# Running sums of squares: which of two engines adds them, in a two-layer decoder trunk

## The chip, the core and the metric

The kernel runs on one core of a Trainium2 chip. The metric is the device time of one launch in microseconds (us). A core has five engines with instruction streams of their own: PE (TensorE, the matmuls), DVE (VectorE), ACT (ScalarE), POOL (GpSimd) and SP (SyncE, which here only issues transfers). Each executes its own instructions in order, and they meet only at semaphores: an instruction raises a counter when it ends, and another engine waits until the counter has reached a number.

## The reference, cut to what matters

The input x has 512 tokens of 1024 features, and there is a memory of 256 tokens. Both layers do the following, where every `rms_norm` divides each token by the root of the mean of its 1024 squares (plus 1e-6) and multiplies by a gain:

```python
for l in range(2):
    h = rms_norm(x, norm_mix_pre[l])             # "mix_pre"
    y = concat(mla(h), mlstm(h), dilated_swa(h)) @ w_out[l]
    x = x + rms_norm(y, norm_mix_post[l])        # "mix_post"
    h = rms_norm(x, norm_x_pre[l])               # "x_pre"
    y = memory_cross_attention(h, rms_norm(mem, norm_mem[l]), x_w_q[l], x_w_kv[l], x_w_o[l])
    x = x + rms_norm(y, norm_x_post[l])          # "x_post"
    h = rms_norm(x, norm_ffn_pre[l])             # "ffn_pre"
    y = swiglu(h, w_gate_up[l], w_down[l])
    x = x + rms_norm(y, norm_ffn_post[l])        # "ffn_post"
```

The six norms with a name in the comments are the ones of this case, in two layers: twelve norms of 1024 features.

## The kernel before, in words

**Layout.** Activations are kept feature-major: x is eight tiles (KT = 8) of 128 features (the partitions) by 512 tokens. Every weight matrix comes as units of 128 x 1024 f32 (512 KB), 128 units per layer, through a ring of four buffers (RING = 4). For each unit SP loads `raw`, ACT writes a rounded copy `w_hi` (L872), DVE writes the rest `w_lo` = raw - w_hi (L1207), and PE makes three matmuls per product (hi by hi, hi by lo, lo by hi: L504 to L506). A unit's `w_hi` can be written once PE has used the unit four before it. Activations are split in the same way into `h_hi` (ACT) and `h_lo` (DVE).

**The sum of squares of a norm.** For each of its eight tiles ACT squares the tile into `sq`, which has two buffers (`square`, L886 to L891). Before it writes one, it waits until the square two before has been added (`squares_added`, L890). DVE keeps the running sum `acc` (`add_square`, L1179 to L1189): a copy for the first tile (L1186) and an addition of two 128 x 512 f32 tiles in SBUF for the other seven (L1188). DVE then waits for its own result (`done`). When all eight are in, PE multiplies `acc` by a matrix of ones, which sums over the features (`norm_sum`, L545 to L552), and ACT makes `rstd` of it with a logarithm and an exponential (`make_rstd`, L900 to L909).

**Where the twelve sums stand.** In each layer:

- "mix_post" is summed while PE makes the eight tiles of the output projection ("out"); DVE norms the memory in the same loop (L1559). PE's `norm_sum` stands behind the first tile of the next projection ("xk").
- "x_pre": when rstd of mix_post is there, DVE scales a tile of y (L1267) and adds the tile before to x (L1271), then makes one `w_lo` (L1565), then adds the square of the tile before that (L1567). PE meanwhile makes the xk tiles and the first four units of "xv" with matmuls of 256 columns or with two token blocks; `norm_sum("x_pre")` stands behind the fourth xv unit (L793). ACT, in its own order for tile m (L1120 to L1126): `w_hi` of unit m + 3, `k_x` of tile m, the square of tile m - 3. The `w_hi` of the fourth xv unit comes behind the last square (L1127).
- "x_post" is summed during the eight tiles of "xo", and "ffn_post" during the eight of "down". In both PE's `norm_sum` stands directly behind the last tile (L821, L856), and four matmuls without use follow (`keep_busy`, L563), save at the kernel's end.
- "ffn_pre" (`ffn_input`, L1597) and, for the second layer, "mix_pre" (`next_input`, L1633) follow them: per tile DVE does y (L1267), x (L1271), `h_lo` of the tile before (L1194), the square's addition. PE takes each tile as soon as its `h_lo` is there (`after_norm`, L568): 12 matmuls per tile in front of ffn_pre, 9 in front of mix_pre (L580 to L582).

**The other users.** In the feed-forward part `acc` and `sq` hold other data (L328). POOL does nothing in the kernel but one copy per layer (L495), which it makes when the last numerator of the mLSTM has been computed.

Of the kernel before, what the change touches and what calls it, by code (L numbers as in the profile page):

```python
# [23 lines left out]
DEPTH = 2  # L24
# [232 lines left out]
def build(nc, x_in, mem_in, w_in, g_in, c_in, out):  # L257
    with ExitStack() as ctx:
# [199 lines left out]
        with nc.Block() as block:  # L458
# [31 lines left out]
            @block.gpsimd  # L490
            def _(pool):
                for layer in range(DEPTH):
                    pool.wait_ge(k_pe_ready, count(k_pe_ready, layer, 1))
                    pool.wait_ge(ml_num, count(ml_num, layer, ML_HEADS * TB))
                    pool.tensor_copy(k_mla[K_PE_ROWS[0], 2:MLA_HEADS, :], k_pe[K_PE_ROWS[0], :].unsqueeze(1)  # L495
                                     .broadcast_to([MLA_ROPE, MLA_HEADS - 2, SEQ])).then_inc(k_pe_copied, 1)

            @block.tensor
# [674 lines left out]
            def _(dve):  # L1173
# [5 lines left out]
                def add_square(layer, name, k):  # L1179

                    c = layer * N_SQUARES + squares_before(name) + k
                    dve.wait_ge(squared, c + 1)
                    if k == 0:
                        if layer or NORM_AT[name]:
                            dve.wait_ge(norm_summed, count(norm_summed, layer, NORM_AT[name]))
                        ins = dve.tensor_copy(acc[:, :], sq[:, c % 2, :])  # L1186
                    else:
                        ins = dve.tensor_tensor(acc[:, :], acc[:, :], sq[:, c % 2, :], ALU.add)  # L1188
                    done(ins, squares_added)  # L1189
# [30 lines left out]
                for layer in range(DEPTH):  # L1220
                    def gain(col, rows=slice(0, P)):
                        return gains[rows, layer, col:col + 1]

                    def add_squares(name, n, between=None, beside=lambda k: None):
                        for k in range(n):
                            beside(k)
                            add_square(layer, name, k)
                            if between is not None:
                                between(k)
# [314 lines left out]
                    for s in range(PAIR_STEPS + PAIR_LAG + 2):  # L1544
# [9 lines left out]
                        if t >= 2 and t % TB == 1:  # L1554
# [3 lines left out]
                    mem_norm = (KT, tiles(mem), G_MEM, tiles(m_hi), tiles(m_lo))  # L1558
                    add_squares("mix_post", KT, between=lambda m: norm_step("mem", m, *mem_norm),  # L1559
                                beside=lambda m: lo_until(U_OUT + m + 4))  # L1560
                    norm_step("mem", KT, *mem_norm)
                    
                    def x_square(k):

                        lo_until(U_XK + k + 4)  # L1565
                        if k >= 1:
                            add_square(layer, "x_pre", k - 1)  # L1567

                    residual("mix_post", "out", y_x, x_square)
                    add_square(layer, "x_pre", KT - 1)  # L1570
                    lo_until(U_XV + 7)
# [12 lines left out]
                    def x_lo(head):  # L1584
                        for c in range(2):
# [7 lines left out]
                              lambda h: X_HD ** -0.5, x_lo)  # L1593
                    add_squares("x_post", KT, beside=lambda m: lo_until(U_XO + m + 4))
                    lo_until(U_FF + RING)

                    def ffn_input(k):  # L1597

                        if k >= 1:
                            scaled_lo(layer, "ffn_pre", k - 1, G_FFN_PRE)  # L1600
                            add_square(layer, "ffn_pre", k - 1)

# [5 lines left out]
                    for p in range(FT):  # L1608
# [20 lines left out]
                    dve.wait_ge(ff_lo, count(ff_lo, layer, FT))  # L1629
                    add_squares("ffn_post", KT, beside=lambda m: lo_until(  # L1630
                        USES[use_of("down", m)][0][-1][0] + RING))

                    def next_input(k):  # L1633

                        if k >= 1 and layer + 1 < DEPTH:
                            scaled_lo(layer + 1, "mix_pre", k - 1, G_MIX_PRE)
                            add_square(layer + 1, "mix_pre", k - 1)
                        if k == 3:
# [134 lines left out]
```

## Time and profile before

| what | value |
|---|---|
| median of 3 runs | 1725.98 us (1724.89 to 1728.15) |
| span of the profiled execution | 1726.0 us, first to last instruction |
| PE busy | 1632.5 us, 95% |
| DVE busy | 959.1 us, 56% |
| ACT busy | 723.5 us, 42% |
| POOL busy | 5.7 us, 0% (6 instructions) |
| loads | 141.31 MB read, 83 GB/s over the span |

The page names an instruction group by its line, engine, operation and tiles, as `acc<-acc,sq` for an addition of `sq` to `acc`. Behind an arrow in square brackets stands how long the engine sat idle before the instruction and which instruction ended that. The profile's span stands for the execution's own time here: it lies 0.02 us above the median.

### The profile page before, as it was taken

What the parts mean: (1) busy time and instruction counts of PE and PEld (TensorE: products, weight loads), DVE (VectorE), ACT (ScalarE), POOL (GpSimd) and SP (SyncE); (2) the same over time, 40 slices, a digit from 0 to 9 for tenths busy, and PEclk for the clock granted to TensorE, in tenths of its full rate; (3) what the DMA queues carried; (4) which work ended last, traced back from release to release, by engine and by line L of the source; (5) the groups of instructions that cost most, each with busy time, mean ns of one, the idle gap of its engine ahead of it and who ended that gap; (6) DMA issues with size and microseconds to landing.
All of it is one profiled execution on the core that took longest, in us unless ns stands there. A gap on an engine that the chain in (4) does not pass through costs nothing.

```text
span 1726.0 us, 19043 instructions
## 1 busy us (share of the span) xinstructions
PE 1632.5 (95%) x7260; PEld 1254.5 (73%) x7260; DVE 959.1 (56%) x1492; ACT 723.5 (42%) x1208; POOL 5.7 (0%) x6
## 2 busy tenths in 40 slices
PE   7999899999999999999989998899999999999996
PEld 5765557877668888888767555587768688888884
DVE  5768764764365555532286677557553755555323
ACT  5522654544344444432244227445343444444321
POOL 0000000000000000000000000000000000000000
PEclk9998999999999999999999889999999999999998
DMA  5321003341213333333213110134302123333321
GB/s 227 109 61 37 13 1 122 115 154 49 62 49 98 98 99 107 99 110 98 85 54 106 48 37 1 42 105 147 122 25 86 58 89 100 106 101 98 110 73 49
DMA packets 38826, 144.64 MB, mean 84 GB/s; under 512 B 4304, under 2 KB 4432, under 8 KB 38224
## 3 DMA queue, kind: packets, MB, share of 16 engines
q1 hardware_dynamic: 38736, 143.43, 26.0%
q8 instruction: 58, 0.95, 0.2%
q14 instruction: 32, 0.26, 0.0%
HBM read 141.31 MB, written 2.10 MB: 83 GB/s over the span
## 4 chain that ended last, share of the span: by engine, by line
PE 84%; DVE 8%; ACT 5%; issue 3%; DMA 0%; SPq 0%; DVEq 0%; ACTq 0%
PE bank L504 24%; PE bank L506 24%; PE bank L505 24%; PE bank L756 2%; PE bank L813 2%; PE bank L731 2%; PE bank L803 1%; PE bank L657 1%; PE bank L665 1%; PE bank L744 1%; DVE x L1271 1%; ACT p_mix L1091 1%; DVE tn_x L1236 1%; DVE w_lo L1207 1%; PE bank L551 1%
## 5 line engine op out<-in xcount | busy, mean ns | idle before, releaser
L504 PE MATMUL bank<-h_hi,w_hi 128*128 128x512 f32 x1312 | 528.5, 403 | 34.6 <-DVE h_lo L1194 15.4
L1207 DVE TENSOR_TENSOR w_lo<-raw,w_hi 128x1024 fp32r<-128x1024 f32 x256 | 312.7, 1225 | 435.3 <-ACT w_hi L872 422.4
L505 PE MATMUL bank<-h_lo,w_hi 128*128 128x512 f32 x1312 | 516.3, 393 | 0.0
L506 PE MATMUL bank<-h_hi,w_lo 128*128 128x512 f32 x1312 | 515.9, 393 | 0.0
L872 ACT ACTIVATE w_hi<-raw 128x1024 fp32r<-128x1024 f32 x256 | 268.3, 1050 | 194.7 <-PE bank L506 185.6
L504 PEld LDWEIGHTS bank<-h_hi,w_hi 128*128 128x128 f32 x1312 | 249.2, 190 | 106.1 <-issue 23.8
L505 PEld LDWEIGHTS bank<-h_lo,w_hi 128*128 128x128 f32 x1312 | 249.5, 190 | 54.0 <-issue 3.4
L506 PEld LDWEIGHTS bank<-h_hi,w_lo 128*128 128x128 f32 x1312 | 249.5, 190 | 53.0
L504 PE MATMUL bank<-a_hi,w_hi 128*128 128x512 f32 x352 | 136.9, 389 | 0.0
L505 PE MATMUL bank<-a_lo,w_hi 128*128 128x512 f32 x352 | 136.9, 389 | 0.0
L506 PE MATMUL bank<-a_hi,w_lo 128*128 128x512 f32 x352 | 136.9, 389 | 0.0
L1188 DVE TENSOR_TENSOR acc<-acc,sq 128x512 f32<-128x512 f32 x84 | 58.0, 691 | 102.4 <-ACT sq L891 101.3
L891 ACT ACTIVATE sq<-bank 128x512 f32<-128x512 f32 x48 | 28.7, 598 | 153.4 <-PE bank L506 153.4
L1163 ACT ACTIVATE a_hi<-sq 128x512 fp32r<-128x512 f32 x44 | 27.8, 632 | 140.8 <-DVE sq L1621 140.8
L506 PEld LDWEIGHTS bank<-a_hi,w_lo 128*128 128x128 f32 x352 | 66.1, 188 | 13.8
L505 PEld LDWEIGHTS bank<-a_lo,w_hi 128*128 128x128 f32 x352 | 66.1, 188 | 13.7
L504 PEld LDWEIGHTS bank<-a_hi,w_hi 128*128 128x128 f32 x352 | 66.1, 188 | 13.6
L1158 ACT ACTIVATE acc<-sq 128x512 f32<-128x512 f32 x44 | 27.8, 632 | 110.1 <-DVE sq L1614 110.1
L1010 ACT ACTIVATE w_ml<-w_ml 128x512 f32<-128x512 f32 (+3 forms) x32 | 15.0, 470 | 114.9 <-DVE w_ml L1437 114.9
L731 PE MATMUL bank<-k_mla,q_mla 128*128 128x128 f32 (+3 forms) x128 | 43.2, 463 | 5.3 <-DVE stat L1530 5.3
L504 PE MATMUL bank<-m_hi,w_hi 128*128 128x256 f32 x128 | 38.0, 297 | 5.6 <-DVE w_lo L1207 4.9
L1540 DVE COPY pt_mix<-bank 128x128 f32<-128x128 f32 (+3 forms) x48 | 23.6, 491 | 32.4 <-PE bank L744 31.1
(191 smaller groups left out, 1935.3 us busy)
## 6 DMA issues: line engine op xcount, KB each, us to landing
raw<-w_in SPq DMA_DIRECT2D x256, 512.0 KB, 3.5
x<-x_in SPq DMA_DIRECT2D x4, 512.0 KB, 7.3
mem<-mem_in SPq DMA_DIRECT2D x2, 1024.0 KB, 5.2
out<-x SPq DMA_DIRECT2D x4, 512.0 KB, 2.6
consts<-c_in SPq DMA_DIRECT2D x1, 1728.0 KB, 13.1
mem_sq<-mem_in SPq DMA_DIRECT2D x1, 1024.0 KB, 7.7
gains<-g_in SPq DMA_DIRECT2D x1, 80.0 KB, 3.4
```

Source lines behind the costliest of these rows:

```text
L504: pe.matmul(out_ap, l_hi, r_hi, start=start, stop=False)
L505: pe.matmul(out_ap, l_hi, r_lo, start=False, stop=False)
L506: return pe.matmul(out_ap, l_lo, r_hi, start=False, stop=stop)
L731: pe.matmul(score_ring[u % 4][:, 0:n], hd["q"][:, qb * P:n], hd["k"][:, 0:n], start=True, stop=True).then_inc(mix_at["scored"], 1)
L756: mm = pe.matmul(outs[pair % 2][64 * i:64 * i + 64, kb * P:SEQ], mix_head(2 * pair + i)["v"](kb), pt_mix[:, i, kb, kb * P:SEQ], start=(kb ...
L813: mm = pe.matmul(outs[c][:, :], v_x[:, kb, col:col + P], pt_x[:, head % 2, kb, :], start=(kb == 0), stop=(kb == 1))
L872: act.activation(w_hi[:, s, :], raw[:, s, :], ACT.Copy).then_inc(split_hi, 1)
L891: act.activation(sq[:, c % 2, 0:width], src, ACT.Square).then_inc(squared, 1)
L1158: done(act.activation(sig, gate_up, ACT.Exp, scale=-1.0), act_step)
L1163: act.activation(a_hi[:, p * SEQ:(p + 1) * SEQ], gate_up, ACT.Copy).then_inc(ff_hi, 1)
L1188: ins = dve.tensor_tensor(acc[:, :], acc[:, :], sq[:, c % 2, :], ALU.add)
L1207: dve.tensor_tensor(w_lo[:, s, :], raw[:, s, :], w_hi[:, s, :].bitcast(F32), ALU.subtract)\
```

## The change

POOL gets a function `add_squares(layer, name)` that makes the copy and the seven additions of one norm into `acc`, each raising `squares_added` as before. It waits for `squared` before each, for the `norm_summed` of the norm before in front of the copy, and for its own addition before the next. POOL's program per layer becomes: its one copy of `k_mla` as before, then the sums of mix_post, x_pre, x_post, ffn_pre, ffn_post, and, in the first layer, mix_pre of the second. DVE keeps `add_square` for mix_pre of the first layer alone; all its other calls are gone, and its loops keep the rest of their work in the same order. 88 instructions move: 77 additions and 11 copies. No semaphore, buffer or transfer is added or removed, and ACT and PE are as they were.

```diff
--- before.py
+++ after.py
@@ -489,11 +489,31 @@
 
             @block.gpsimd
             def _(pool):
+                added = [KT]
+
+                def add_squares(layer, name):
+
+                    for k in range(KT):
+                        c = layer * N_SQUARES + squares_before(name) + k
+                        pool.wait_ge(squared, c + 1)
+                        if k == 0:
+                            pool.wait_ge(norm_summed, count(norm_summed, layer, NORM_AT[name]))
+                            ins = pool.tensor_copy(acc[:, :], sq[:, c % 2, :])
+                        else:
+                            pool.wait_ge(squares_added, added[0])
+                            ins = pool.tensor_tensor(acc[:, :], acc[:, :], sq[:, c % 2, :], ALU.add)
+                        ins.then_inc(squares_added, 1)
+                        added[0] += 1
+
                 for layer in range(DEPTH):
                     pool.wait_ge(k_pe_ready, count(k_pe_ready, layer, 1))
                     pool.wait_ge(ml_num, count(ml_num, layer, ML_HEADS * TB))
                     pool.tensor_copy(k_mla[K_PE_ROWS[0], 2:MLA_HEADS, :], k_pe[K_PE_ROWS[0], :].unsqueeze(1)
                                      .broadcast_to([MLA_ROPE, MLA_HEADS - 2, SEQ])).then_inc(k_pe_copied, 1)
+                    for name in ("mix_post", "x_pre", "x_post", "ffn_pre", "ffn_post"):
+                        add_squares(layer, name)
+                    if layer + 1 < DEPTH:
+                        add_squares(layer + 1, "mix_pre")
 
             @block.tensor
             def _(pe):
@@ -1181,8 +1201,6 @@
                     c = layer * N_SQUARES + squares_before(name) + k
                     dve.wait_ge(squared, c + 1)
                     if k == 0:
-                        if layer or NORM_AT[name]:
-                            dve.wait_ge(norm_summed, count(norm_summed, layer, NORM_AT[name]))
                         ins = dve.tensor_copy(acc[:, :], sq[:, c % 2, :])
                     else:
                         ins = dve.tensor_tensor(acc[:, :], acc[:, :], sq[:, c % 2, :], ALU.add)
@@ -1221,10 +1239,9 @@
                     def gain(col, rows=slice(0, P)):
                         return gains[rows, layer, col:col + 1]
 
-                    def add_squares(name, n, between=None, beside=lambda k: None):
+                    def beside_squares(n, between=None, beside=lambda k: None):
                         for k in range(n):
                             beside(k)
-                            add_square(layer, name, k)
                             if between is not None:
                                 between(k)
 
@@ -1556,18 +1573,15 @@
 
                     dve.wait_ge(mem_loaded, count(mem_loaded, layer, 16))
                     mem_norm = (KT, tiles(mem), G_MEM, tiles(m_hi), tiles(m_lo))
-                    add_squares("mix_post", KT, between=lambda m: norm_step("mem", m, *mem_norm),
-                                beside=lambda m: lo_until(U_OUT + m + 4))
+                    beside_squares(KT, between=lambda m: norm_step("mem", m, *mem_norm),
+                                   beside=lambda m: lo_until(U_OUT + m + 4))
                     norm_step("mem", KT, *mem_norm)
                     
                     def x_square(k):
 
                         lo_until(U_XK + k + 4)
-                        if k >= 1:
-                            add_square(layer, "x_pre", k - 1)
 
                     residual("mix_post", "out", y_x, x_square)
-                    add_square(layer, "x_pre", KT - 1)
                     lo_until(U_XV + 7)
                     dve.wait_ge(rstd_ready, count(rstd_ready, layer, NORM_AT["x_pre"] + 1))
                     for k in range(KT + 1):
@@ -1591,14 +1605,13 @@
 
                     attention(x_at, X_HEADS, p_x, lambda qb: N_MEM, lambda h: C_CAUSAL - (SEQ - N_MEM),
                               lambda h: X_HD ** -0.5, x_lo)
-                    add_squares("x_post", KT, beside=lambda m: lo_until(U_XO + m + 4))
+                    beside_squares(KT, beside=lambda m: lo_until(U_XO + m + 4))
                     lo_until(U_FF + RING)
 
                     def ffn_input(k):
 
                         if k >= 1:
                             scaled_lo(layer, "ffn_pre", k - 1, G_FFN_PRE)
-                            add_square(layer, "ffn_pre", k - 1)
 
                     residual("x_post", "xo", y_x, ffn_input)
                     ffn_input(KT)
@@ -1627,14 +1640,13 @@
                         dve.tensor_tensor(a_lo[:, at], gate_up, a_hi[:, at].bitcast(F32), ALU.subtract)\
                            .then_inc(ff_lo, 1)
                     dve.wait_ge(ff_lo, count(ff_lo, layer, FT))
-                    add_squares("ffn_post", KT, beside=lambda m: lo_until(
+                    beside_squares(KT, beside=lambda m: lo_until(
                         USES[use_of("down", m)][0][-1][0] + RING))
 
                     def next_input(k):
 
                         if k >= 1 and layer + 1 < DEPTH:
                             scaled_lo(layer + 1, "mix_pre", k - 1, G_MIX_PRE)
-                            add_square(layer + 1, "mix_pre", k - 1)
                         if k == 3:
                             lo_until(N_UNITS + RING)
 
```

## Rows read from the trace of the kernel before

**Rows 1.** The page: span, busy time, and the chain that ended last by engine.

```profile
span 1726.0 us, 19043 instructions
PE 1632.5 (95%) x7260; PEld 1254.5 (73%) x7260; DVE 959.1 (56%) x1492; ACT 723.5 (42%) x1208; POOL 5.7 (0%) x6
...
PE 84%; DVE 8%; ACT 5%; issue 3%; DMA 0%; SPq 0%; DVEq 0%; ACTq 0%
```

**Rows 2.** Tile acc: ns min/median/max, first, last start; then idle us, times behind it.

```profile
L1188 DVE TENSOR_TENSOR acc<-acc,sq x84: 683/692/694, 9.0 to 1709.0; 128x512 f32<-128x512 f32 x84
...
L1186 DVE COPY acc<-sq x12: 427/428/428, 7.8 to 1604.2; 128x512 f32<-128x512 f32 x12
...
  DVE acc L1188: 13.1, 8
```

**Rows 3.** Timeline around POOL's first copy: start us, us, engine, line, op.

```profile
179.49 2.74 POOL L495 COPY k_mla<-k_pe 32x3072 f32<-32x3072 f32 x1 [179.06 <-PE bank L665]
180.15 0.69 DVE L1367 TENSOR_TENSOR q_mla<-bank,consts 128x512 f32<-128x512 f32 x1 [0.92 <-PE bank L506]
```

**Rows 4.** Timeline of the stage of x_pre in layer 0, DVE.

```profile
314.50 1.29 DVE L1267 TENSOR_TENSOR y_x<-y_x,rstd 128x512 f32<-128x512 f32 x2 [3.01 <-ACT rstd L909]
330.64 0.69 DVE L1267 TENSOR_TENSOR y_x<-y_x,rstd 128x512 f32<-128x512 f32 x1
...
331.97 1.23 DVE L1207 TENSOR_TENSOR w_lo<-raw,w_hi 128x1024 fp32r<-128x1024 f32 x1
333.11 0.69 DVE L1188 TENSOR_TENSOR acc<-acc,sq 128x512 f32<-128x512 f32 x1
...
344.65 4.63 DVE L1207 TENSOR_TENSOR w_lo<-raw,w_hi 128x1024 fp32r<-128x1024 f32 x4
```

**Rows 5.** Timeline of the same stage, PE: its waits and the sum of x_pre.

```profile
311.02 0.39 PE L504 MATMUL bank<-m_hi,w_hi 128*128 128x256 f32 x1 [0.24 <-DVE m_lo L1241]
...
325.83 0.36 PE L504 MATMUL bank<-m_hi,w_hi 128*128 128x256 f32 x1 [1.26 <-DVE w_lo L1207]
...
333.34 0.36 PE L504 MATMUL bank<-m_hi,w_hi 128*128 128x256 f32 x1 [1.21 <-DVE w_lo L1207]
...
340.75 0.50 PE L504 MATMUL bank<-w_hi,m_hi 128*128 128x512 f32 x1 [1.30 <-DVE w_lo L1207]
...
349.08 1.02 PE L551 MATMUL bank<-acc,consts 128*128 128x512 f32 x2
```

**Rows 6.** Timeline at the end of xo, layer 0: from the last square to rstd.

```profile
486.40 0.60 ACT L891 ACTIVATE sq<-bank 128x512 f32<-128x512 f32 x1 [3.32 <-PE bank L506]
...
487.03 0.69 DVE L1188 TENSOR_TENSOR acc<-acc,sq 128x512 f32<-128x512 f32 x1 [2.62 <-ACT sq L891]
...
487.78 1.12 PE L551 MATMUL bank<-acc,consts 128*128 128x512 f32 x2 [1.41 <-DVE acc L1188]
```

**Rows 7.** Timeline of the stage of ffn_pre in layer 1, DVE and PE.

```profile
1347.36 0.47 PE L504 MATMUL bank<-h_hi,w_hi 128*128 128x512 f32 x1 [2.14 <-DVE h_lo L1194]
...
1349.04 0.75 DVE L1194 SCALAR_TENSOR_TENSOR h_lo<-x,gains,h_hi 128x512 fp32r<-128x512 f32 x1
...
1351.88 0.75 DVE L1194 SCALAR_TENSOR_TENSOR h_lo<-x,gains,h_hi 128x512 fp32r<-128x512 f32 x1
...
1367.49 1.02 PE L551 MATMUL bank<-acc,consts 128*128 128x512 f32 x2
```

**Rows 8.** Windows in that stage, layer 0; granted clock is third from the end.

```profile
496.00:498.00 2.00, 2.00 (x6) 1.58 (x5) 1.90 (x4) 1.25 (x2) 0.00 (x0) 0.50 0.04 8
500.00:502.00 2.00, 2.00 (x10) 1.62 (x9) 1.93 (x4) 0.40 (x2) 0.00 (x0) 1.00 0.00 0
```

**Rows 9.** Timeline of the stage of layer 1's mix_pre, PE.

```profile
874.17 0.50 PE L504 MATMUL bank<-h_hi,w_hi 128*128 128x512 f32 x1 [1.62 <-DVE h_lo L1194]
...
879.86 0.50 PE L504 MATMUL bank<-h_hi,w_hi 128*128 128x512 f32 x1 [0.50 <-DVE h_lo L1194]
...
886.32 1.02 PE L551 MATMUL bank<-acc,consts 128*128 128x512 f32 x2
```

## The prediction

> **What bounds the kernel now.** I read the page first. PE is busy for 95% of 1726.0 us and makes 84% of the chain that ended last; POOL has 5.7 us of work [rows 1]. So a busy second of DVE is worth nothing in itself. What matters is where PE waits for something in which the sums of squares have a part, and I went through the timelines of those places. There are four kinds.
>
> First, the ends of xo and down, two in each layer. PE has nothing else to do there, and its wait for acc is on the chain: square, addition, matmul of ones [rows 6]. The four such waits of PE and of its weight loads are all waits that acc ever caused PE, 13.1 us in both together [rows 2]. The other eight sums are finished before PE asks for them.
>
> Second, the stage of x_pre, twice. PE would need 2.78 us per unit (its last three before the sum, 340.75 to 349.08), DVE's loop takes longer, and PE waits three times for w_lo: 1.26 + 1.21 + 1.30 = 3.8 us [rows 5]. In DVE's loop the addition stands between one w_lo and the next, and a step without it is 330.64 to 333.11, 2.47 us [rows 4]. What PE gets back there is passed on, since the norm and the q projection behind it hang on the sum of x_pre.
>
> Third, the stage of ffn_pre, twice. DVE's step from h_lo to h_lo is 1349.04 to 1351.88, 2.84 us, and PE goes through it without a wait after its start: 20.13 us from 1347.36 to 1367.49 for 87 matmuls (7 steps of 12 and three of the next), 0.231 us each or 2.78 us a step [rows 7]. DVE and PE are level. In layer 0 PE is itself slower for a moment: it ran at half the granted clock, 1.2 GHz, around 497 us, after an idle stretch, and 2.4 GHz again from about 500 us [rows 8]. That leaves it some 1.6 us behind DVE (eight matmuls at 0.43 instead of 0.23 us).
>
> Fourth, the stage of mix_pre of layer 1, once. PE needs 9 matmuls, 2.05 to 2.08 us, per step against DVE's 2.84, waits in most steps (1.62 us where DVE makes a w_lo between them), and the wait of 0.50 us at 879.86 is the last [rows 9].
>
> **What moves, and its price on each engine.** 77 additions at 0.69 us and 11 copies at 0.43 us leave DVE [rows 2], 58 us of busy time. Nothing else moves; no transfer and no queue of SP is concerned. On POOL no addition is seen. The one kind of work it has takes 2.74 us for 3072 elements per partition, 0.89 ns each, for one operand read [rows 3]. By that a copy of 512 is 0.46 us. An addition is 0.91 us if the two operands are read one after the other, and 1.37 us if the write counts like a read. I take the middle, 1.14 us, and keep 0.91 and 1.37 for the range. (The Trainium skill, GPSIMD Engine Reference, Performance versus the Vector engine, gives 4497 ns for an f32 addition of 2048 elements, of which a quarter is an estimate of 1.12 us; by that the sum below would be some 0.4 us less. No row here shows it.) DVE takes up its wait for a square within 0.03 us (486.40 + 0.60 to 487.03) [rows 6]; for POOL I allow 0.1 us.
>
> **Does POOL's addition cost DVE time?** This decides the sign, and the trace is silent. A DVE copy from SBUF of 512 elements takes 0.43 us, an addition 0.69 us [rows 2]: the difference, 0.26 us, is half of 512 elements at 0.96 elements per ns (which is w_lo's 1.23 us less 0.69 us for 512 more). DVE thus has two ways of reading SBUF, and an addition of two SBUF tiles uses both. Beside POOL's copy a DVE instruction kept its 0.69 us, but it read one operand from a PSUM bank and left a way free [rows 3]. In the stages that count, all of y, x, h_lo and w_lo read two SBUF tiles. The bounds are no delay at all and the whole of each addition, 1.14 us. I take the whole, since the overlap that was seen is the one kind that a shared way would allow. A rule speaks for this and against the change: the Trainium skill, SBUF — State Buffer, Who interferes with whom, says that a DVE instruction with two SBUF inputs and a GpSimd one that reads SBUF exclude each other for their full length. By it the sum is the forecast's; without it, the first rival's.
>
> **The sum, with blocking.**
> - Ends of xo and down: 1.14 + 0.1 - 0.69 = 0.55 us later each, four times [rows 6]: +2.2 us. DVE's next w_lo needs a w_hi that ACT makes behind the square and y, so it starts later and the two hardly meet.
> - x_pre: DVE no longer waits for squares. From 314.50, eight steps of 2.47, one y (0.61) and the ninth w_lo (1.23) are 21.6 us; the additions take 0.5 + 7 x 1.14 = 8.5 us of the same ways [rows 4]. The w_lo of the fourth xv unit is then ready at 344.6 instead of 345.9, its w_hi standing behind the last square in ACT's order. One unit of PE later (2.78 us) the sum of x_pre stands at 347.4 to 347.8 instead of 349.08 [rows 5]: 1.5 us earlier, twice: -3.0 us.
> - ffn_pre: a DVE step is 2.84 - 0.72 + 1.14 = 3.26 us, and in the first one a copy and an addition come together, +1.2 us. Over h_lo 1 to 5 that is 1.2 + 4 x 0.42 = 2.9 us, after which DVE has no more y and runs ahead. Layer 1, where PE is level: +3.0 us. Layer 0, where PE is 1.6 us behind: +1.4 us [rows 7, 8].
> - mix_pre of layer 1: DVE bounds it up to the last step, +3.3 us [rows 9].
> - mix_post and all that lies in front of the last tiles of out, xo and down: nothing; a tile of 24 matmuls takes PE 5.5 us there, and the square, an addition on POOL (1.24 us) and a w_lo (1.23 us) fit beside it even one after the other. If they did not, each w_lo missed would cost PE up to 1.2 us. PE's wait for the last m_lo in front of xk (0.24 us [rows 5]) may go too, 0.3 us in both layers together.
>
> Sum: 2.2 - 3.0 + 3.0 + 1.4 + 3.3 - 0.3 = +6.6 us, 1726.0 + 6.6 = 1732.6 us. The profiled span is 1726.0 and the median 1725.98, so nothing has to be converted. With 0.91 us for the addition the terms are 1.3 - 6.6 + 2.0 + 2.0, or 1724 to 1725 us; with 1.37 us they are 3.1 + 0.2 + 6.6 + 4.7, or 1741 us.
>
> **Rivals.**
> 1. *No blocking; faster.* The mechanism's place is the stage of x_pre: DVE's step becomes 2.47 us, under PE's 2.78, and the three waits for w_lo go, -3.8 us twice [rows 4, 5]. In mix_pre of layer 1 DVE's step falls to 2.12 us, about PE's 2.05: -3.5 us [rows 9]. ffn_pre gives 0.2 us at most, PE being level. The ends still cost 2.2 us, the m_lo waits give 0.5. Together -9.4 us, 1716.6 us. For it: POOL's copy delayed nobody [rows 3]. Against: what ran beside it used one way. It decides as soon as an addition costs DVE less than the 0.72 us (0.69 and its gap) that leave it. Chance 0.28.
> 2. *Blocking, and DVE keeps the way through its back-to-back instructions.* POOL then gets in only when DVE idles, ACT stands at its next square (two buffers), and with it h_hi and w_hi. Per two tiles DVE has 4.24 us of work and then waits 1.14 + 0.60 + 0.75 us for an addition, a square [rows 6] and an h_hi (taken as long as an h_lo [rows 7]): 3.37 us a tile instead of 3.26, some +2 us over three stages, and the gain at x_pre is gone, +3 us: 1738 us. For it: DVE's next instruction starts (333.11) before a w_lo has ended (331.97 + 1.23 = 333.20) [rows 4]. Against: x and h_lo are each followed by a wait for their own result, which leaves the way free for a moment. Chance 0.12.
> 3. *Something small in its place*: one more stretch of PE at 1.2 GHz behind the longer idle times (+1.6 us as in layer 0 [rows 8]) or one fewer, or the two halves of the sum cancelling. 1725 to 1728 us. Chance 0.05. That POOL would not do the additions at all has no mechanism; both operands lie in SBUF.
>
> **How the numbers follow.** The forecast has 0.55, and its own range is 1724 to 1741 us, all from the price of one addition. A measurement of this kernel can tell about 0.2%, 3.5 us, from no change: faster is below 1722.5, slower above 1729.4. Of the forecast's 0.55, 0.37 lie above, 0.13 within, 0.05 below; rival 2 is above; rival 1 is below but for 0.01; rival 3 is within for the most part. That makes faster 0.33, same 0.18, slower 0.49. Both signs hold much, so the range reaches from the middle of rival 1 to the forecast's upper end: 1714 to 1740 us.
>
> **What would show it.** DVE's additions to acc fall from 84 to 7 and POOL shows 77, of about 1.1 us by the distance of their starts. Right: in the three stages y, x, h_lo or w_lo instructions of DVE become longer than 0.69 to 1.23 us, or gaps of about 1.1 us appear between them, one per addition; PE's waits for h_lo appear in ffn_pre of layer 1 and grow in mix_pre; the acc waits at the four ends are longer by 0.5 us. Wrong: DVE's durations and gaps beside POOL's additions as before, the three waits for w_lo gone, PE at 2.78 us per unit up to the sum of x_pre. The forecast fails mostly if the blocking isn't whole, and, less, if an addition on POOL is far from 1.14 us.

## The result, and the profile after

The changed kernel takes 1737.44 us (median of 11 runs, 1733.64 to 1743.83) against 1727.09 us for the kernel before in 11 runs beside it: a ratio of 1.0051, 95% interval 1.0035 to 1.0066. It is slower. The forecast was 1732.6 us, 6.6 us above the kernel before, in a range of 1714 to 1740 us; it named the side and the mechanism, and several of its terms were mis-sized. Of all executions told of below one, of the kernel e3, took 3633.72 us, twice the rest, and e3's ratio leaves it out.

First the page of the changed kernel: its span, the busy times, the engines' shares of the chain that ended last, and POOL's new group.

```profile
span 1742.0 us, 19065 instructions
...
PE 1648.1 (95%) x7260; PEld 1259.9 (72%) x7260; DVE 938.7 (54%) x1404; ACT 721.9 (41%) x1208; POOL 124.0 (7%) x94
...
PE 81%; DVE 9%; ACT 5%; issue 4%; DMA 0%; POOL 0%; POOLq 0%; SPq 0%; DVEq 0%; ACTq 0%
...
L504 POOL TENSOR_TENSOR acc<-acc,sq 128x512 f32<-128x512 f32 x77 | 110.9, 1441 | 353.6 <-ACT sq L911 352.8
```

DVE had 959.1 us of work before [rows 1] and has 938.7 now. It gave away 58 us and got back 38: its remaining instructions have become longer. The tile acc in the changed kernel (least, median and greatest duration in ns, first and last start):

```profile
L504 POOL TENSOR_TENSOR acc<-acc,sq x77: 1262/1299/2380, 283.2 to 1723.5; 128x512 f32<-128x512 f32 x77
L501 POOL COPY acc<-sq x11: 610/615/951, 277.8 to 1618.7; 128x512 f32<-128x512 f32 x11
L1206 DVE TENSOR_TENSOR acc<-acc,sq x7: 691/691/694, 10.7 to 23.2; 128x512 f32<-128x512 f32 x7
```

An addition costs POOL 1.30 us where DVE needed 0.69 [rows 2], a copy 0.61 instead of 0.43. Now DVE and POOL in the stage of ffn_pre of the first layer, from the timeline of the changed kernel (start, duration, instruction, and in square brackets the idle time before it):

```profile
501.83 0.75 DVE L1212 SCALAR_TENSOR_TENSOR h_lo<-x,gains,h_hi 128x512 fp32r<-128x512 f32 x1
502.61 0.69 DVE L1284 TENSOR_TENSOR y_x<-y_x,rstd 128x512 f32<-128x512 f32 x1
503.15 1.30 POOL L504 TENSOR_TENSOR acc<-acc,sq 128x512 f32<-128x512 f32 x1 [1.91 <-ACT sq L911]
503.22 1.78 DVE L1288 TENSOR_TENSOR x<-x,y_x 128x512 f32<-128x512 f32 x1
505.04 0.75 DVE L1212 SCALAR_TENSOR_TENSOR h_lo<-x,gains,h_hi 128x512 fp32r<-128x512 f32 x1
```

The addition to x, 0.69 us elsewhere, lasts 1.78 us beside POOL's. It starts 0.07 us after POOL's addition and ends 0.55 us after that has ended. DVE's step from h_lo to h_lo is 3.21 us; it was 2.84 [rows 7]. The engine that was relieved has become slower. In the stage of x_pre POOL's additions meet longer DVE instructions, and POOL waits as well:

```profile
331.55 1.61 POOL L504 TENSOR_TENSOR acc<-acc,sq 128x512 f32<-128x512 f32 x1 [1.95 <-ACT sq L911]
334.43 1.69 POOL L504 TENSOR_TENSOR acc<-acc,sq 128x512 f32<-128x512 f32 x1 [1.27 <-ACT sq L911]
337.30 2.38 POOL L504 TENSOR_TENSOR acc<-acc,sq 128x512 f32<-128x512 f32 x1 [1.18 <-ACT sq L911]
340.19 7.96 POOL L504 TENSOR_TENSOR acc<-acc,sq 128x512 f32<-128x512 f32 x4 [0.50 <-ACT sq L911]
```

The third starts together with a w_lo of DVE (337.31, 1.23 us) and takes 2.38 us, its own 1.30 and most of the w_lo's length: the exclusion goes both ways. What PE waited for in the changed kernel, over the whole span (total, times, longest):

```profile
PE bank L524 <- DVE h_lo L1212: 19.0, 16, 9.5
PE bank L524 <- DVE w_lo L1225: 8.3, 6, 2.5
PE bank L571 <- POOL acc L504: 8.1, 4, 2.0
```

In the kernel before, the same three waits of PE are 15.4, 11.6 and 5.7 us.

To see where the time came from I cut each execution at the starts of its logarithms (the instructions that make the first rstd of a norm from a bank), and compared the stages between them with those of the kernel before. All in us, each the difference of that stage alone; "mixer" is the attention, mLSTM and output part that ends with the norm of mix_post.

```
stage ending with     layer 0: after  again   layer 1: after  again
start, mix_pre                  2.54   1.38             2.61   2.61
mixer, mix_post                 3.40  -0.67             3.43   0.91
x_pre                          -2.38  -2.35            -2.37  -2.29
cross attention, x_post         1.10   1.18             1.12   1.46
ffn_pre                         1.13   1.16             2.48   2.50
feed-forward, ffn_post          1.47   0.60             1.44   0.53
sum of all, span minus 1726.0: after 16.0, again 7.0
```

"After" is the profile shown above; "again" is a second profile of the same changed kernel (e4 below). What is alike in both belongs to the change: x_pre gives back, and the two ends, ffn_pre and mix_pre of the second layer cost. What differs, the mixer above all, does not: in the first layer no sum is moved in it ahead of its last part. (How ffn_pre's two numbers come to differ is told with the first experiments.) The windows of 2 us of the changed kernel show what it is (busy time of PE, PEld, DVE, ACT and POOL, the granted clock of TensorE, the DMA share and GB/s):

```profile
116.00:118.00 2.00, 2.00 (x3) 0.56 (x3) 0.70 (x2) 1.17 (x2) 0.00 (x0) 0.50 0.00 0
118.00:120.00 2.00, 2.00 (x5) 1.14 (x4) 1.97 (x3) 0.00 (x0) 0.00 (x0) 0.50 0.00 0
```

The same windows of the second profile, in which the mixer starts 1.2 us sooner:

```profile
116.00:118.00 2.00, 2.00 (x8) 1.36 (x8) 1.85 (x3) 0.01 (x1) 0.00 (x0) 1.00 0.00 0
118.00:120.00 2.00, 2.00 (x8) 1.17 (x8) 1.13 (x4) 0.42 (x1) 0.00 (x0) 1.00 0.48 119
```

At 0.50, which is 1.2 GHz, PE starts fewer matmuls in the same 2 us than at 1.00, 2.4 GHz. How often that happens in the mLSTM changes from one execution to the next, and this stage differs from that of the kernel before by -2.3 to +3.4 us in kernels that are nearly alike there. Its length follows the time at 0.50: over all eleven profiles, those of the experiments below included, the first layer's lasts 279.6 to 281.3 us with 24 us at 0.50 and 283.8 us with 34 us, the second layer's 276.2 and 276.7 us with 24 us and 282.0 us with 38 us. The profile of after is that of its slowest run, 1743.83 us, and the second profile, whose mixers have fewer such stretches and whose start is earlier, is 9 us shorter.

### The profile page after: what moved, and what is told of

It reads as the page before. It is cut to its first block, busy times and chain, and to the rows that moved or that the text cites. A ratio compares the mean times of both kernels' runs of the same rounds, so it can differ in the third digit from the quotient of the medians.

```text
span 1742.0 us, 19065 instructions
## 1 busy us (share of the span) xinstructions
PE 1648.1 (95%) x7260; PEld 1259.9 (72%) x7260; DVE 938.7 (54%) x1404; ACT 721.9 (41%) x1208; POOL 124.0 (7%) x94
## 4 chain that ended last, share of the span: by engine, by line
PE 81%; DVE 9%; ACT 5%; issue 4%; DMA 0%; POOL 0%; POOLq 0%; SPq 0%; DVEq 0%; ACTq 0%
PE bank L524 23%; PE bank L525 22%; PE bank L526 22%; DVE x L1288 3%; PE bank L833 2%; PE bank L677 2%; PE bank L776 2%; PE bank L751 2%; PE bank L685 1%; PE bank L823 1%; DVE y_x L1284 1%; ACT p_mix L1111 1%; DVE h_lo L1212 1%; PE bank L764 1%; PE bank L571 1%
## 5 line engine op out<-in xcount | busy, mean ns | idle before, releaser
L1225 DVE TENSOR_TENSOR w_lo<-raw,w_hi 128x1024 fp32r<-128x1024 f32 x256 | 318.7, 1249 | 551.9 <-ACT w_hi L892 539.3
L504 POOL TENSOR_TENSOR acc<-acc,sq 128x512 f32<-128x512 f32 x77 | 110.9, 1441 | 353.6 <-ACT sq L911 352.8
L501 POOL COPY acc<-sq 128x512 f32<-128x512 f32 x11 | 7.4, 674 | 907.9 <-ACT sq L911 907.9
```

The costliest lines, as they stand in the source:

```text
L504: ins = pool.tensor_tensor(acc[:, :], acc[:, :], sq[:, c % 2, :], ALU.add)
L1225: dve.tensor_tensor(w_lo[:, s, :], raw[:, s, :], w_hi[:, s, :].bitcast(F32), ALU.subtract)\
```

## The experiments

Nine kernels ran, those of one letter on one chip beside the kernel before.

### The change taken apart

Four kernels: the norms whose sums go to POOL are a tuple, and DVE keeps the others.

```diff
+            ON_POOL = ("mix_post", "x_pre")            # e1
+            ON_POOL = ("x_post", "ffn_post")           # e2
+            ON_POOL = ("ffn_pre", "mix_pre")           # e3, mix_pre of layer 1 alone
             def add_squares(layer, name):              # POOL
+                if name not in ON_POOL:
+                    return
...
                 def add_square(layer, name, k):        # DVE
+                    if name in ON_POOL and (layer or name != "mix_pre"):
+                        return
```

e4 is the changed kernel again. Expected of e1, e2, e3 and e4:

> POOL sums mix_post and x_pre only (32 of the 88 instructions); DVE keeps the rest. Theory (the change gains in the stage of x_pre and loses at the ends of xo and down and in the stages of ffn_pre and mix_pre): the gain alone is left, two times the 2.4 us seen in the changed kernel at x_pre and two times 0.6 us at mix_post, about 6 us, so 0.35% faster than before (ratio 0.9955 to 0.998). Rival (the additions on POOL cost wherever they run, and the shorter stage of x_pre in the changed kernel was luck): no faster than before, ratio 1.000 or above.

> POOL sums x_post and ffn_post only. Theory: each of the four ends costs the longer addition (1.30 + 0.07 instead of 0.69 + 0.03 us, 0.6 us) and what PE's lower clock behind the longer wait adds; the changed kernel showed 1.1 to 1.5 us each, so 2.4 to 5.6 us slower, ratio 1.0015 to 1.003. Rival (DVE is relieved of 32 additions here too, and w_lo comes sooner): no slower than before.

> POOL sums ffn_pre and layer 1's mix_pre only. Theory (POOL's addition excludes DVE's instructions with two SBUF inputs for its whole length): DVE's x instructions beside an addition take 1.78 us instead of 0.69, a step 3.21 instead of 2.84 us, and PE's waits give 1.4 + 3.0 + 3.3 us, some 6 to 8 us slower, ratio 1.0035 to 1.0045. Rival (the losses in these stages of the changed kernel come from the later rstd and the clock behind the ends, not from the additions): within 0.1% of before.

> The changed kernel once more, for a second profile. In its first one 3.4 us per layer were lost between the norm of kv and the eight tiles of out, where no sum is made and PE ran more often at 1.2 GHz. If that is the luck of an execution, the loss there is smaller or gone in this profile, or appears in the profiles of the other kernels as well, and the sum of the other stages stays at about 6.6 us. If it belongs to the change, it is there again with about 3.4 us in both layers and in no other kernel.

Measured, each against a median of 1730.9 us for the kernel before:

```
kernel                       us        ratio    95% interval
e1 mix_post, x_pre         1726.12    0.9975   0.9963 to 0.9988
e2 the four ends           1733.14    1.0018   1.0007 to 1.0029
e3 ffn_pre, mix_pre (l. 1) 1737.2     1.0036   1.0021 to 1.0052
e4 all, changed kernel     1736.68    1.0034   1.002  to 1.0048
```

The parts add up: -0.0025 + 0.0018 + 0.0036 is +0.0029, and the whole gives +0.0034. In the profiles each part changes its own stages (the mixer and the start apart): e1 x_pre by -2.37 and -2.30; e2 the ends by 1.20, 0.58, 1.18 and 0.54; e3 ffn_pre by 1.13 and 2.46 and mix_pre of the second layer by 2.64. So POOL's sums are a gain in one place and a loss in three, and the loss at ffn_pre and mix_pre, where DVE was relieved of most, is the largest.

One stage moves without its sums having been moved: ffn_pre is 1.33 us longer in e1's second layer and 1.37 shorter in e2's first. The clock again, here the second layer's windows of e1 and then of the kernel before:

```profile
1346.00:1348.00 2.00, 2.00 (x7) 1.57 (x6) 1.93 (x4) 1.24 (x2) 0.00 (x0) 0.56 0.00 0
```

```profile
1346.00:1348.00 2.00, 0.64 (x3) 0.59 (x4) 1.90 (x4) 1.61 (x3) 0.00 (x0) 1.00 0.00 0
```

With DVE's sums and no work on POOL the stage lasts 28.2 us where PE runs at 0.50 over the first of its tiles, and 26.9 us where it does not; five of the ten such stages profiled (the kernel before, e1, e2, f1, g1) are of either kind. With POOL's sums it lasts 29.3 to 29.4 us in all eight profiled, wherever the stretch falls. So the 1.1 us of the first layer and the 2.5 of the second differ by where the stretch fell in the one profile of the kernel before, and not by the layer: the mean is 1.8 us each, with the same sum of 3.6 us.

In e3 the mix_pre stage of the second layer shows the blocking beside each tile (timeline of DVE; the first row an x, the fourth a y):

```profile
873.87 1.77 DVE L1294 TENSOR_TENSOR x<-x,y_f 128x512 f32<-128x512 f32 x1
875.67 0.75 DVE L1217 SCALAR_TENSOR_TENSOR h_lo<-x,gains,h_hi 128x512 fp32r<-128x512 f32 x1
876.46 1.23 DVE L1230 TENSOR_TENSOR w_lo<-raw,w_hi 128x1024 fp32r<-128x1024 f32 x1
877.60 1.78 DVE L1290 TENSOR_TENSOR y_f<-y_f,rstd 128x512 f32<-128x512 f32 x1
```

### Idle work on POOL beside the kernel before

The changed kernel mixes two things, that DVE has less to do and that POOL adds. f2 and f3 are the kernel before, with DVE's sums all where they were, and with work on POOL whose result nobody uses (once per layer, at the last feed-forward tile, DVE waits until it is done): one instruction beside each square of ffn_pre, and one beside each of 18 tiles of the feed-forward part. In f2 it is an addition of two constant tiles, in f3 a memset in the first layer and a copy in the second.

```diff
+                def work(layer):
+                    pool.tensor_tensor(junk, const(...), const(...), ALU.add)    # f2
+                    pool.memset(junk, 0.0)                                       # f3, layer 0
+                    pool.tensor_copy(junk, const(...))                           # f3, layer 1
...
+                    for k in range(KT):
+                        pool.wait_ge(squared, layer * N_SQUARES + squares_before("ffn_pre") + k + 1)
+                        work(layer)
+                    for p in range(FT - 4):
+                        pool.wait_ge(ff_step, count(ff_step, layer, 2 * p + 1 + p % 2))
+                        work(layer)
```

> The kernel before, all sums on DVE; POOL makes additions beside it that nobody waits for, of two constant tiles into an unused one: one per square of ffn_pre, and one beside each of 18 feed-forward tiles. Blocking for the whole length: where one starts while DVE has an instruction with two SBUF inputs next, that one is longer by up to 1.3 us (a step of ffn_pre 2.84 + 1.2 to 1.3 us), and an instruction that reads one operand from a PSUM bank keeps its 0.69 us. Rival (the two engines share bandwidth and both slow down a little, or the longer x instructions of the changed kernel waited for data, not for the port): DVE's instructions are all longer by a like share, or none is.

> As the run before, but POOL's idle work is a memset (which reads nothing) in layer 0 and a copy (one operand read) in layer 1. If it is the reading that excludes DVE: no longer DVE instruction beside the memsets, and ones longer by up to 0.6 us beside the copies. If any work of POOL on SBUF excludes DVE: longer ones in both layers. If it takes two operands on both sides: none in either.

f2 took 1741.52 us and f3 1733.95 us, one run each, beside 1730.83 us before; with one run, the total of f3 says nothing, and I go by stages and rows. The stages of ffn_pre are longer by 5.29 and 6.62 us in f2, 33.5 us in both layers; in f3 by nothing in the first layer (-0.03, memsets) and by 1.95 in the second (copies). That second stage has a stretch at 0.50 over its first tiles, which the kernel before has not: of the 1.95 us such a stretch alone brings up to 1.3, and 0.6 at least are the copies'. The timeline of f2, first in ffn_pre, then in the feed-forward part:

```profile
502.65 1.29 POOL L497 TENSOR_TENSOR pt_x<-consts 128x512 f32<-128x512 f32 x1 [3.04 <-ACT sq L915]
502.77 1.72 DVE L1291 TENSOR_TENSOR y_x<-y_x,rstd 128x512 f32<-128x512 f32 x1
...
540.24 0.69 DVE L1645 TENSOR_TENSOR sq<-bank,acc 128x512 f32<-128x512 f32 x1
540.35 1.29 POOL L497 TENSOR_TENSOR pt_x<-consts 128x512 f32<-128x512 f32 x1 [5.97 <-DVE acc L1643]
...
550.01 0.69 DVE L1643 TENSOR_TENSOR acc<-acc,rstd 128x512 f32<-128x512 f32 x1
550.12 1.74 POOL L497 TENSOR_TENSOR pt_x<-consts 128x512 f32<-128x512 f32 x1 [8.48 <-DVE acc L1642]
550.73 0.69 DVE L1645 TENSOR_TENSOR sq<-bank,acc 128x512 f32<-128x512 f32 x1
```

Three cases stand here side by side. A DVE multiplication of two SBUF tiles that starts 0.12 us behind POOL's addition takes 1.72 us instead of 0.69. One whose first operand is a PSUM bank (540.24) keeps its 0.69 us beside POOL, and POOL its 1.29. And where DVE's two-tile instruction was first (550.01), POOL's addition starts inside it and takes 1.74 us, 0.45 more than 1.29: POOL waits for DVE's. The 18 idle additions per layer in the feed-forward part cost that stage only 0.24 and 0.23 us; PE bounds it, and DVE has idle time there. The timeline of f3, a memset in the first layer and a copy in the second:

```profile
501.75 0.53 POOL L503 MEMSET pt_x<- 128x512 f32 x1 [2.05 <-ACT sq L915]
501.90 0.69 DVE L1291 TENSOR_TENSOR y_x<-y_x,rstd 128x512 f32<-128x512 f32 x1
...
1355.26 0.61 POOL L500 COPY pt_x<-consts 128x512 f32<-128x512 f32 x1 [2.56 <-ACT sq L915]
1355.40 1.01 DVE L1291 TENSOR_TENSOR y_x<-y_x,rstd 128x512 f32<-128x512 f32 x1
```

The memset only writes, and DVE loses nothing; the copy reads, and DVE's instruction ends 0.54 us after the copy has, just as x ended 0.55 us after the addition above. The others are alike. In ffn_pre of f3 all eight two-tile DVE instructions that start behind a memset keep their length and all eight behind a copy are 0.27 to 0.38 us longer; in f2 all eight y behind an addition are 1.01 or 1.02 us longer, and all 18 DVE instructions with a PSUM operand that start behind one keep theirs. So it is POOL's reading of SBUF that keeps a two-tile DVE instruction out until POOL's has ended. The rule that the prediction cited from the Trainium skill, SBUF — State Buffer, Who interferes with whom, is that a DVE instruction with two SBUF inputs contends with a GpSimd one that reads SBUF, and not with one that only writes. The trace agrees, with 1.72 us for 0.69 beside the addition and 0.69 beside the memset.

### Where the gain at x_pre comes from

The changed kernel gains 2.35 us per layer at x_pre. That is either because 8 instructions left DVE, or because DVE no longer waits there for ACT's square. f1 has no work on POOL. DVE makes all additions as before, but in the stage of x_pre each one tile later:

```diff
                     def x_square(k):
                         lo_until(U_XK + k + 4)
-                        if k >= 1:
-                            add_square(layer, "x_pre", k - 1)
+                        if k >= 2:
+                            add_square(layer, "x_pre", k - 2)
...
+                    add_square(layer, "x_pre", KT - 2)
                     add_square(layer, "x_pre", KT - 1)
```

> The kernel before, with no sum on POOL; in the stage of x_pre DVE adds each square one tile later (88 instructions, the same work). Theory (what the changed kernel gained at x_pre is that DVE no longer waits for ACT's squares, 4.7 us in both layers of the kernel before, and not the 0.72 us of work per tile): most of the gain is there, x_pre 1.5 to 2.4 us earlier in each layer, 3 to 5 us in all, ratio 0.997 to 0.9985. Rival (the work taken off DVE is the gain): DVE has as much to do as before and x_pre gains under 0.5 us per layer.

f1 took 1720.11 us beside 1730.83: 0.9939, 0.9924 to 0.9955. It is faster than both kernels, and by more than expected. Its x_pre stages are shorter by 4.71 and 4.64 us, twice what the changed kernel gets and 9.4 of the 10.7 us. DVE's timeline in f1:

```profile
332.40 1.23 DVE L1207 TENSOR_TENSOR w_lo<-raw,w_hi 128x1024 fp32r<-128x1024 f32 x1
333.55 0.69 DVE L1188 TENSOR_TENSOR acc<-acc,sq 128x512 f32<-128x512 f32 x1
334.27 0.69 DVE L1267 TENSOR_TENSOR y_x<-y_x,rstd 128x512 f32<-128x512 f32 x1
334.88 0.68 DVE L1271 TENSOR_TENSOR x<-x,y_x 128x512 f32<-128x512 f32 x1
335.60 1.23 DVE L1207 TENSOR_TENSOR w_lo<-raw,w_hi 128x1024 fp32r<-128x1024 f32 x1
```

From w_lo to w_lo 3.20 us, back to back, with the addition in it: 2.47 us for the three other instructions [rows 4] and 0.73. In the kernel before this loop was not slow by its work alone; DVE stood waiting for squares. Its waits there, between 313 and 350 us (not shown above):

```profile
DVE acc L1186 <- ACT sq L891: 2.6, 1, 2.6
DVE acc L1188 <- ACT sq L891: 2.1, 2, 1.0
```

Together 4.7 us, and f1 gets back 4.71. PE's waits for w_lo in the same stage, the changed kernel (313 to 353 us) and then f1 (313 to 350 us):

```profile
PEld bank L524 <- DVE w_lo L1225: 3.0, 2, 1.6
...
PE bank L524 <- DVE w_lo L1225: 2.1, 2, 1.2
```

```profile
PEld bank L504 <- DVE w_lo L1207: 0.5, 1, 0.5
```

The changed kernel waits for no square on DVE and makes no addition there, and still gains only half as much: the other half went to POOL's reads, which are the long instructions of DVE in this stage (a w_lo of 2.19 us at 340.87 us in the trace of after, 1.23 otherwise). Eight of DVE's y, x and w_lo there are longer than alone, by 7.8 us together in each layer; f1's copy and seven additions take 5.5 us of DVE with their gaps. The difference is 2.3 us, and f1's stage is 2.3 us the shorter.

g1 is f1 with one more such move: in the loop of mix_post the memory norm's step stands in front of the addition, so that the square has longer to arrive.

```diff
                     def add_squares(name, n, between=None, beside=lambda k: None):
                         for k in range(n):
                             beside(k)
-                            add_square(layer, name, k)
                             if between is not None:
                                 between(k)
+                            add_square(layer, name, k)
```

> The run with the later additions on DVE (0.9939 of before), and in the loops of mix_post DVE makes the step of the memory's norm before it waits for the square. Theory (the 0.6 us by which mix_post came earlier with its sum on POOL is PE no longer waiting for the last m_lo behind DVE's wait for a square): the same 0.6 us per layer without POOL, 1 us more than in that run, ratio 0.993 to 0.994. Rival (it was POOL's part that brought it): no difference at mix_post.

g1 took 1720.34 us beside 1729.68: 0.9949, 0.9936 to 0.9963. Expected was 1 us less than in f1; the interval overlaps f1's, so the move can't be told from nothing in the total. In the profile the time from the last square of mix_post to its logarithm falls from 4.40 to 3.78 us, and it is 3.81 in the changed kernel. The same 0.6 us are there with POOL and without it.

### Why the ends cost more than an addition

At the end of xo and down the addition is 0.61 us longer than on DVE, but two of the four ends cost 1.1 to 1.5 us. g3 is the changed kernel with two matmuls without use in front of each of these sums, so that PE is not idle while it waits for POOL:

```diff
+                    keep_busy(2)
                     norm_sum("x_post")
...
+                    keep_busy(2)
                     norm_sum("ffn_post")
```

> The changed kernel with two more matmuls without use (about 0.9 us each) in front of the sums of x_post and ffn_post, so that PE is not idle while POOL adds the last square. Theory (of the 1.1 to 1.5 us that these ends lost in the changed kernel, 0.6 us is the longer addition, and the rest is that PE's clock falls to 1.2 GHz during the longer wait, 2.0 us instead of 1.4): the ends lose 0.6 us each with the granted clock at 1.00 behind them, the kernel is some 1 to 2 us faster than the changed one, ratio to before 1.002 to 1.004. Rival (all of the loss is POOL's addition and its latency): the ends stay at 1.1 us or more; if the useless matmuls outlast the addition, more.

g3 took 1733.51 us: 1.0019, 1.001 to 1.0028. Its interval overlaps that of e4, so what the two matmuls bring is read from the stages. Its four ends cost 0.64, 0.60, 0.58 and 0.54 us. Timeline and window of the end of xo, first in e4, then in g3:

```profile
486.77 1.67 PE L571 MATMUL bank<-acc,consts 128*128 128x512 f32 x2 [2.03 <-POOL acc L504]
```

```profile
488.00:490.00 2.00, 2.00 (x4) 0.73 (x3) 0.29 (x2) 1.32 (x2) 0.00 (x0) 0.50 0.44 74
```

```profile
486.76 1.12 PE L571 MATMUL bank<-acc,consts 128*128 128x512 f32 x2 [0.32 <-POOL acc L504]
```

```profile
488.00:490.00 2.00, 2.00 (x6) 0.89 (x5) 0.83 (x3) 1.24 (x2) 0.00 (x0) 1.00 0.32 80
```

Both reach the sum at the same time (486.77 and 486.76), so the two extra matmuls delay nothing. But in e4 PE sat idle for 2.03 us before it, the granted clock then stood at 0.50, 1.2 GHz, and its two matmuls took 1.67 us instead of 1.12. In the kernel before the wait was 1.41 us [rows 6], and the clock was 1.00, 2.4 GHz, in its window of 488 to 490 us. The longer addition costs 0.6 us, and the fall of the clock behind the longer wait 0.5 to 0.9 more, at x_post in both layers and, in the profile of after, at ffn_post. This is no chance of one profile. In after, e2 and e4 the wait is 2.02 or 2.03 us at all twelve ends, and the sum's two matmuls take 1.5 to 2.1 us at eight of them, all six of xo and two of the six of down. In g3, and in the seven kernels whose ends DVE sums (waits of 1.41 to 1.49 us), they take 1.12 or 1.13 us at all 32. In g3 a stretch at 0.50 comes later, at 494.2 us in the first layer, in the stage of ffn_pre, which stays at 29.3 us. Why the clock held at four ends of down was not tried.

## Why the prediction was right, and where its sizes were off

The terms as predicted, and as the stages of e4 show them (all parts moved, and fewest slow stretches):

```
term                     predicted   measured
four ends                   +2.2      +3.8   (1.18 + 0.60 + 1.46 + 0.53)
x_pre, two layers           -3.0      -4.6
ffn_pre                     +4.4      +3.7   (1.16 + 2.50)
mix_pre of layer 1          +3.3      +2.6
mix_post                    -0.3      -1.2   (0.6 a layer, last square to logarithm)
sum                         +6.6      +4.3
```

The last term lies in a stage whose clock wanders by more than its size; that it reaches the end of the kernel is not shown. Without it the measured sum is +5.5 us, a ratio of 1.0032, near e4's 1.0034. All terms are taken against one profile of the kernel before. The intervals of the two measured ratios, 1.0051 and 1.0034, share 1.0035 to 1.0048, which is 6.1 to 8.3 us of 1730; the predicted +6.6 lies in it, partly by luck, since its errors have opposite signs.

**Blocking.** Right, and decisive. Rival 1 wanted an addition to cost DVE less than 0.72 us; it costs 1.03 to 1.09 (1.72 and 1.78 less 0.69). f2 shows it without any other change. Where nothing hides the loss and DVE saves nothing, the stage of ffn_pre grows by 6.6 us.

**The price of an addition.** "I take the middle, 1.14 us" was too low: 1.30 us, near the upper bound of 1.37 that was kept. The copy was 0.61 instead of 0.46. Full exclusion with this price would make DVE's step 2.84 - 0.72 + 1.30 = 3.42 us. It is 3.21, since x starts 0.07 us behind POOL's addition and ends 0.55 us behind its end, not 0.69: 1.09 us are lost, not 1.30. That brings the step back to near the 3.26 that was predicted. The estimate from the page of the Trainium skill, GPSIMD Engine Reference, Performance versus the Vector engine, was 1.12 us; the 1.30 us of these rows decide. With a size of 512 elements the quarter of its figure for 2048 was too low.

**ffn_pre and mix_pre.** Mechanism right; +2.5 instead of +3.0 and +2.6 instead of +3.3, a little high, of which the step's growth of 0.37 us instead of 0.42 is 0.2 us; the rest was not traced. The lower loss in the first layer, where PE had been behind after its stretch at 1.2 GHz [rows 8], came as predicted (+1.2 instead of +1.4). But it belongs to that profile, not to the layer: in e1 the second layer has the stretch too, in f1 the second alone.

**The ends.** The failed step is "1.14 + 0.1 - 0.69 = 0.55 us later each". The addition itself gives 0.6 us, as g3 shows, but a term was missing: a longer wait of PE can also cost it its clock. The prediction knew the effect from rows 8 and put it with the small stuff of rival 3, at 1.6 us; it belonged in the sum of the ends, where PE had already been idle for 1.41 us.

**x_pre.** The failed step is "1.5 us earlier": it was 2.35. The step charged every POOL addition to DVE in full, 8.5 us at its price of 1.14; at the measured 1.30 that would have been 9.7. In the rows above POOL starts beside a w_lo and is itself the one that waits (1.61 to 2.38 us for an addition of 1.30), so DVE lost less, 7.8 us. And the cause of the gain was named only in passing, "DVE no longer waits for squares", with no row for it: those waits are 4.7 us, and f1 shows that they alone are worth 4.7 us per layer, with all additions kept on DVE. Rival 1 put the whole gain, with the additions gone as well, at 3.8.

**Rival 2.** The half of it that is true is that POOL waits behind DVE where DVE is back to back. Starvation did not follow: POOL's eight additions in that stage end in time, and in ffn_pre DVE's step is 3.21 us and not the 3.37 it asked for.

**Against which time.** "Nothing has to be converted" was not quite right: in the profiles whose own time is known, the time is 1.8 to 2.1 us above the span, 1743.83 for 1742.0. The profile of before, at 1726.0, belongs to a run near 1727.8 us, and its start was 1.4 to 2.6 us earlier than that of every later profile. It shifts no term of the sum. Two slips change nothing either: by the shares given for each rival, faster adds up to 0.32 and same to 0.19, and the lower end of the range, 1714 us, lies below the 1716.6 of rival 1 that it is said to be.

**Open.** Why the mixer's clock differs from one execution to the next was not tried. Nor was a kernel that keeps POOL's sums of x_pre but shifts them away from DVE's two-tile instructions; f1 leaves little to gain by it here.

## What to carry to other kernels

Before work is moved to POOL, look at what DVE will do beside it: if those are instructions with two SBUF tiles, a POOL instruction that reads SBUF costs DVE nearly its whole length, here 1.03 to 1.09 us of 1.30 where it came first, for each 0.69 us taken away, while memsets, and DVE instructions with a PSUM operand, run side by side. If an engine is late, see first whether it works or waits: putting each addition of x_pre one tile later in DVE's own order (f1) gave 0.9939 [0.9924, 0.9955], where moving them and those of mix_post to the other engine (e1) gave 0.9975 [0.9963, 0.9988], and moving all 1.0051. And where PE already idles before a dependent matmul, price a longer wait with the clock it may lose; two matmuls without use in front of each sum cut the four ends from +3.8 to +2.4 us.

## What the runs showed of the hardware that I had not expected

- The exclusion is in both directions, and the profile books it as duration: POOL's additions are 1.27 us alone (the last of xo in e4, at 485.45 us), up to 2.38 us beside DVE; there is no idle gap to see, the instruction is just longer.
- A one-operand DVE copy is held back too. Beside an idle addition of POOL in f2, and an h_lo in front of it, its timeline shows a copy at 1.39 us that takes 0.43 in f3:

```profile
496.66 1.81 DVE L1218 SCALAR_TENSOR_TENSOR h_lo<-x,gains,h_hi 128x512 fp32r<-128x512 f32 x1
498.50 1.39 DVE L1210 COPY acc<-sq 128x512 f32<-128x512 f32 x1
```

  A rule by the number of operands would have let it pass; at 0.43 us for 512 elements it reads 1.2 elements per ns, more than the 0.96 of one way [rows 2, 4], so it may use both. No run tests that.
- On POOL a memset of 512 elements per partition takes 0.53 us, a copy 0.61 and an addition 1.30: the addition costs twice a copy, not the 1.5 times that one more operand would suggest.
- The same kernel's mixer can differ by several us between executions through the clock alone (windows at 0.50 and 1.00 above, on identical code). A stage table of one profile against one other needs a second profile before a stage of a few us is believed.
